# Retention in three fp32r passes, and the turn of the PSUM banks moved behind held values, in a two-block mixer

## What is computed

```python
p = h @ w_in                                  # q, k, v and gate of every head
q_l, k_l = rope(q_l), rope(k_l)               # latent tokens only
o_c, s_f, s_b = retention_bidir(q_c, k_c, v_c, lg_f, lg_b, zeros, zeros)
o_l, _, _     = retention_bidir(q_l, k_l, v_l, lg_f, lg_b, s_f, s_b)
# retention: out_n = sum_m gamma^|n-m| (q_n . k_m) v_m, forward and backward
on = o * rsqrt(mean(o * o) + EPS)             # per head, over the 512 values
y  = (on * norm_gain * silu(g)) @ w_out
```

## Time and profile before

| | before |
|---|---|
| median of three runs | 3357.47 us (3341.77 to 3360.63) |
| the profiled execution | 3363.55 us |
| its span | 3362.2 us |
| mean granted clock of TensorE | 0.988 of 2.4 GHz |
| busy: TensorE, VectorE, ScalarE | 3257.1, 1705.7, 1263.1 us |
| moved by DMA | 508.93 MB, mean 151 GB/s |
| retention heads | about 206 to 1830 us of the span |

### The profile page before, as it was taken

The page is one execution under the profiler, slowest core; times in us unless marked ns, Lnnn a source line. Parts: engine busy times, 40 slices in busy tenths (PEclk is TensorE's granted clock), DMA queues, the critical chain, the costliest instruction groups (busy, mean ns, idle before and its releaser), DMA issues.

```text
span 3362.2 us, 47886 instructions
## 1 busy us (share of the span) xinstructions
PE 3257.1 (97%) x20354; PEld 2788.5 (83%) x20354; DVE 1705.7 (51%) x2481; ACT 1263.1 (38%) x1803; POOL 0.2 (0%) x4
## 2 busy tenths in 40 slices
PE   7999999999999999999998999999999999999998
PEld 5677777777777777787875789988999999999998
DVE  5443443334334343443335567778676665555555
ACT  4342222222222222222223455556554444444443
POOL 0000000000000000000000000000000000000000
PEclk9999999999999999999998999999999999999999
DMA  9844423233332233323234234444545545555554
GB/s 371 307 157 182 163 100 131 89 125 125 109 129 94 107 119 114 131 107 113 107 113 163 94 125 139 151 138 158 197 165 173 175 154 166 173 186 189 185 187 144
DMA packets 153923, 508.93 MB, mean 151 GB/s; under 512 B 15344, under 2 KB 35952, under 8 KB 152944
## 3 DMA queue, kind: packets, MB, share of 16 engines
q1 hardware_dynamic: 149328, 493.03, 42.3%
q10 hardware_dynamic: 4384, 12.85, 1.0%
HBM read 501.62 MB, written 4.19 MB: 150 GB/s over the span
## 4 chain that ended last, share of the span: by engine, by line
PE 91%; DVE 3%; ACT 2%; DMA 2%; issue 1%; SPq 1%; ACTq 0%; DVEq 0%
PE bank L543 27%; PE bank L545 27%; PE bank L544 26%; PE bank L605 3%; PE bank L704 2%; PE bank L789 1%; DMA raw<-stream 1%; PE bank L770 1%; PE bank L690 1%; DVE w_lo L1561 1%; PE bank L706 1%; DMA raw_h<-stream 1%; SPq L516 1%; PE bank L780 1%; PE bank L621 0%
## 5 line engine op out<-in xcount | busy, mean ns | idle before, releaser
L543 PE MATMUL bank<-h_hi,w_hi 128*128 128x256 f32 (+1 forms) x4032 | 1271.2, 315 | 10.0 <-DVE w_lo L1561 9.5
L545 PE MATMUL bank<-h_hi,w_lo 128*128 128x256 f32 (+1 forms) x4032 | 1248.4, 310 | 0.0
L544 PE MATMUL bank<-h_lo,w_hi 128*128 128x256 f32 (+1 forms) x4032 | 1248.3, 310 | 0.0
L1561 DVE TENSOR_TENSOR w_lo<-raw,w_hi 128x1024 fp32r<-128x1024 f32 x731 | 885.3, 1223 | 659.7 <-ACT w_hi L1011 654.7
L1011 ACT ACTIVATE w_hi<-raw 128x1024 fp32r<-128x1024 f32 x731 | 764.2, 1057 | 976.4 <-PE bank L545 595.3
L543 PEld LDWEIGHTS bank<-h_hi,w_hi 128*128 128x128 f32 x4032 | 759.4, 188 | 83.9 <-issue 34.7
L545 PEld LDWEIGHTS bank<-h_hi,w_lo 128*128 128x128 f32 x4032 | 763.9, 189 | 43.5
L544 PEld LDWEIGHTS bank<-h_lo,w_hi 128*128 128x128 f32 x4032 | 761.7, 189 | 45.7 <-issue 3.6
L543 PE MATMUL bank<-w_hi,h_hi 128*128 128x512 f32 x704 | 289.6, 411 | 22.1 <-DVE w_lo L1561 9.4
L545 PE MATMUL bank<-w_hi,h_lo 128*128 128x512 f32 x704 | 278.4, 395 | 0.0
L544 PE MATMUL bank<-w_lo,h_hi 128*128 128x512 f32 x704 | 277.9, 395 | 0.0
(11 more groups left out here) (234 smaller groups left out, 2698.8 us busy)
## 6 DMA issues: line engine op xcount, KB each, us to landing
raw<-stream SPq DMA_DIRECT2D x904, 512.0 KB, 4.1
raw_h<-stream SPq DMA_DIRECT2D x32, 512.0 KB, 11.1
res<-tokens_in ACTq DMA_DIRECT2D x4, 1024.0 KB, 8.8
vg<-mem_in ACTq DMA_DIRECT2D x4, 512.0 KB, 9.1
h_hi<-mem_kv ACTq DMA_DIRECT2D x2, 1024.0 KB, 9.9
out<-res SPq DMA_DIRECT2D x4, 512.0 KB, 3.0
mem_kv<-qk ACTq DMA_DIRECT2D x1, 1024.0 KB, 4.8
mem_kv<-vg ACTq DMA_DIRECT2D x1, 1024.0 KB, 11.2
```

The source lines that it names most:

```text
L543: pe.matmul(out, sh, mh, start=start, stop=False)
L544: pe.matmul(out, sh, ml, start=False, stop=False)
L545: return pe.matmul(out, sl, mh, start=False, stop=stop)
L1561: dve.tensor_tensor(in_quarters(m.w_lo[slot][:, :]), m.raw[SLOT[raw]], in_quarters(m.w_hi[slot][:, :]).bitcast(F32), ALU.subtract).then_in ...
```

## The change

The class `Banks` gets a method that drops several held banks and sets the turn behind the last of them. It is used for all held values:

```diff
+    def drop_all(self, what, tiles):
+        for t in range(tiles):
+            self.drop(*what, t)
+        self.turn = self.values[(*what, tiles - 1)][0] + 1
...
-            for t in range(4):
-                banks.drop("v", h + 1, t)
+            banks.drop_all(("v", h + 1), 4)
```

Queries, keys, scores and values of the retention are split into high and low parts, and their products go through `product`. On TensorE:

```diff
-        pe.wait_ge(*s["roped"].at(h, 3))
+        pe.wait_ge(*s["q_lo"].at(h, 3))
         for mt in range(2):
+            keys = slice(L + mt * P, L + (mt + 1) * P)
             for dt in range(2):
-                mm = pe.matmul(outs[mt][:, :], m.qk[:, 2 + dt, L + mt * P:L + (mt + 1) * P], m.qk[:, dt, :],
-                               start=dt == 0, stop=dt == 1)
+                mm = product(outs[mt][:, :], (m.q_hi[:, 2 + dt, keys], m.q_lo[:, 2 + dt, keys]),
+                             (m.q_hi[:, dt, :], m.q_lo[:, dt, :]), dt == 0, dt == 1)
...
         def outputs_of_head():
-            pe.wait_ge(*banks.at("s", h, 2))
+            pe.wait_ge(*s["s_lo"].at(h, "lat"))
             pe.wait_ge(*banks.at("v", h, 3))
...
-                    pe.matmul(out[:, :], m.v[:, 2 + mt, dv], m.s_ctx[:, mt, :], start=mt == 0, stop=mt == 1)
+                    product(out[:, :], (m.v_hi[:, 2 + mt, dv], m.v_lo[2 + mt][:, dv]),
+                            (m.s_ctx_hi[:, mt, :], m.s_ctx_lo[:, mt, :]), mt == 0, mt == 1)
...
-                    mm = pe.matmul(out[:, LAT], m.v[:, mt, dv], m.s_lat[:, mt, :], start=False, stop=mt == 1,
-                                   skip_group_check=True)
+                    mm = product(out[:, LAT], (m.v_hi[:, mt, dv], m.v_lo[mt][:, dv]),
+                                 (m.s_lat_hi[:, mt, :], m.s_lat_lo[:, mt, :]), False, mt == 1, skip_group_check=True)
```

The latent scores change in the same way as those of the context. On ScalarE, the high parts:

```diff
+    def values_high(h):
+        act.wait_ge(s.mm, WHERE["v", h][7] + 1)
+        for t in range(4):
+            act.activation(m.v_hi[:, t, :], psum("v", h, t)[:, :], ACT.Copy).then_inc(*s["v_hi"].up(h, t))
...
+        def query_high(j):
+            act.wait_ge(*s["roped"].at(h, j))
+            act.activation(m.q_hi[:, j, :], m.qk[:, j, :], ACT.Copy).then_inc(*s["q_hi"].up(h, j))
         for j in range(4):
             ahead(("qk", h, j))
             swap((h, j), m.tmp[j % 2], m.qk[:, j, LAT], 64, banks.at("qk", h, j))
             beside(h, "t", j)
+            if j:
+                query_high(j - 1)
+        query_high(3)
...
         for j in range(3):
+            if j == 2:
+                for mt in range(2):
+                    act.wait_ge(*banks.at("s", h, mt))
+                    act.activation(m.s_ctx_hi[:, mt, :], m.s_raw[:, mt, :], ACT.Copy).then_inc(*s["s_hi"].up(h, mt))
+                act.wait_ge(*banks.at("s", h, 2))
+                act.activation(m.s_lat_hi[:, :, :], m.s_lat_raw, ACT.Copy).then_inc(*s["s_hi"].up(h, "lat"))
             tanh(("g", h, j), m.g[:, j, :], BOTH)
```

On VectorE, the low parts; the value banks are now given free by them:

```diff
+    def values_low(h):
+        for t in range(4):
+            dve.wait_ge(*s["v_hi"].at(h, t))
+            dve.tensor_tensor(m.v_lo[t][:, :], psum("v", h, t)[:, :], m.v_hi[:, t, :].bitcast(F32), ALU.subtract
+                              ).then_inc(*banks.up("v", h, t))
...
+        def query_low(j):
+            dve.wait_ge(*s["q_hi"].at(h, j))
+            dve.tensor_tensor(m.q_lo[:, j, :], m.qk[:, j, :], m.q_hi[:, j, :].bitcast(F32), ALU.subtract
+                              ).then_inc(*s["q_lo"].up(h, j))
...
+        dve.wait_ge(*banks.at("s", h, 2))
+        for mt in range(2):
+            dve.wait_ge(*s["s_hi"].at(h, mt))
+            dve.tensor_tensor(m.s_ctx_lo[:, mt, :], m.s_raw[:, mt, :], m.s_ctx_hi[:, mt, :].bitcast(F32), ALU.subtract
+                              ).then_inc(*s["s_lo"].up(h, mt))
+        dve.wait_ge(*s["s_hi"].at(h, "lat"))
+        dve.tensor_tensor(m.s_lat_lo[:, :, :], m.s_lat_raw, m.s_lat_hi[:, :, :].bitcast(F32), ALU.subtract
+                          ).then_inc(*s["s_lo"].up(h, "lat"))
```

`query_low(j - 1)` stands after the rotation of tile j, `query_low(3)` after the loop, `values_low(h + 1)` after the eight value chunks. In `normed_of_head` the four normalizations no longer stand before the four low parts; the low part of tile j comes two normalizations behind:

```diff
-            for j in range(4):
-                dve.tensor_tensor(m.g[:, j, :], m.g[:, j, :], m.o_rstd[:, :], ALU.mult).then_inc(*s["o_normed"].up(h, j))
-            for j in range(4):
-                dve.wait_ge(*s["o_hi"].at(h, j))
...
+            for j in range(6):
+                if j < 4:
+                    dve.tensor_tensor(m.g[:, j, :], m.g[:, j, :], m.o_rstd[:, :], ALU.mult).then_inc(*s["o_normed"].up(h, j))
+                if j >= 2:
+                    dve.wait_ge(*s["o_hi"].at(h, j - 2))
```

More of the change, by code:

```diff
@@ L335 @@
     "bias1", "squared", "sq_sum", "meaned", "rstd", "h_raw", "h_mod", "h_hi", "h_lo", "mv_turned",
-    "swapped", "roped", "decay_arg", "decay_exp", "decay", "tanh", "gate", "scored", "weighed",
+    "swapped", "roped", "q_hi", "q_lo", "s_hi", "s_lo", "v_hi", "decay_arg", "decay_exp", "decay", "tanh", "gate", "scored", "weighed",
     "o_out", "o_squared", "o_summed", "o_meaned", "o_normed", "o_hi", "o_lo", "added",
@@ L391, in __init__ @@
         self.tab = sb("tab", [P, TABLES_N])
+        v_lo_at += [nc.sbuf_base + 4 * T * i for i in range(3)]
         self.sq = [sb(f"sq{i}", [P, T]) for i in range(2)]
@@ L418, in __init__ @@
         self.o_lo = sb("o_lo", [P, 4, T], F32R, line=128)
-        self.tmp = [sb(f"tmp{i}", [P, L]) for i in range(2)]
+        tmps = sb("tmps", [P, 2, L], line=64)
+        tmp_at = at[0] - 4 * 2 * L
+        self.tmp = [tmps[:, i, :] for i in range(2)]
         self.o_rstd = sb("o_rstd", [P, T])
@@ L430, in __init__ @@
         self.raw += [x[:, 4 * i:4 * i + 4, LAT] for x in self.raw_h for i in range(4)]
-        self.v, self.g = self.vg[:, 0:4, :], self.vg[:, 4:8, :]
+        self.g = self.vg[:, 4:8, :]
+        self.q_hi, self.q_lo = [nc.alloc_sbuf_tensor_at(f"q_{x}", [P, 4, T], F32R, offset=o_at + 4 * 4 * T * i)
+                                for i, x in enumerate(("hi", "lo"))]
+        self.s_ctx_hi = nc.alloc_sbuf_tensor_at("s_ctx_hi", [P, 2, T], F32R, offset=s_at)
+        self.s_ctx_lo = nc.alloc_sbuf_tensor_at("s_ctx_lo", [P, 2, T], F32R, offset=decay_at)
+        self.s_lat_lo = nc.alloc_sbuf_tensor_at("s_lat_lo", [P, 2, L], F32R, offset=tmp_at)
+        self.v_hi = nc.alloc_sbuf_tensor_at("v_hi", [P, 4, RET_DV], F32R, offset=vg_at)
+        self.v_lo = [nc.alloc_sbuf_tensor_at(f"v_lo{t}", [P, RET_DV], F32R, offset=x) for t, x in enumerate(v_lo_at)]
+        self.s_raw, self.s_lat_raw = self.qk[:, 0:2, :], self.qk[:, 2, :].rearrange("p (a b) -> p a b", a=2)
         self.mem_raw = self.vg[:, :, :].rearrange("p a (b c) -> p (a b) c", c=L)
@@ L539, in weights, with product @@
         return m.w_hi[Q[c] % SLOTS], m.w_lo[Q[c] % SLOTS]
-    def product(out, stat, moving, start, stop):
+    def product(out, stat, moving, start, stop, **checks):
         (sh, sl), (mh, ml) = stat, moving
-        pe.matmul(out, sh, mh, start=start, stop=False)
-        pe.matmul(out, sh, ml, start=False, stop=False)
-        return pe.matmul(out, sl, mh, start=False, stop=stop)
+        pe.matmul(out, sh, mh, start=start, stop=False, **checks)
+        pe.matmul(out, sh, ml, start=False, stop=False, **checks)
+        return pe.matmul(out, sl, mh, start=False, stop=stop, **checks)
     def tile(what, cols, k_tiles=KT, k0=0, acts=None, between=None):
@@ L664, in tensor_program @@
                 mean("x0", BOTH)
-        for t in range(2):
-            banks.drop("mv", n, t)
+        banks.drop_all(("mv", n), 2)
     outs = values_banks(("v", 0), 4)
@@ L675, in tensor_program @@
         beside("start", "v", c)
-    for t in range(4):
-        banks.drop("v", 0, t)
+    banks.drop_all(("v", 0), 4)
     for h in range(RET_HEADS):
@@ L895, in tensor_program @@
                 mm.then_inc(*s["meaned"].up("x2_means"))
-        for t in range(2):
-            banks.drop("bv", n, t)
+        banks.drop_all(("bv", n), 2)
     pe.wait_ge(*s["h_lo"].at(2, KT - 1))
@@ L1766, in vector_program @@
             beside(h, "t", 4 + j)
+        dve.wait_ge(*s["q_lo"].at(h, 3))
         dve.wait_ge(*s["scored"].at(h, "ctx"))
```

41 lines of the change are left out of this document (24 added, 17 removed).

## The result

| | before | changed |
|---|---|---|
| median of seven runs | 3357.47 us (3341.77 to 3362.00) | 3321.64 us (3304.12 to 3330.62) |
| ratio | | 0.9887, 95% interval 0.9865 to 0.9909 |
| the profiled execution's span | 3362.2 us | 3320.3 us |
| busy: TensorE, VectorE, ScalarE | 3257.1, 1705.7, 1263.1 us | 3227.0, 1759.7, 1294.9 us |

What follows compares the result with a forecast made beforehand. TensorE's passes plus its few standstills were taken as the bound. Products 24.8 us and bank turn 9.7 gave 34.5 us off 3363.55, so 3329.0, scaled to a median of 3323 us; range 3307 to 3345.

Steps and rivals of the forecast that it cites:

- The pace of the passes: Scores and outputs: three fp32r passes replace each fp32 product, 12.38 us a head for 15.48, saving 24.8 us in eight heads.
- The rule that a quarter would fall away: Scores and outputs: dropping one of four passes would alone save 3.87 us a head, 31.0 us in all.
- The turn: Start of output projections: moving the bank turn past dropped value banks removes seven waits of 1.38 us, saving 9.7 us.
- rival (a): Bank turn gives nothing, as other waits replace those on the values' copies: 24.8 us saved, 3333 us; chance 0.12.
- The parts on ScalarE and VectorE: Seven more copies and eleven subtractions a head cost 0; the queue at the scores has 7.7 us of cover.
- signs of being wrong: New TensorE waits on w_lo inside heads, q_lo or s_lo, 256-column passes above 0.13 us, or a third-pair projection wait.
- v(0): Wait of 5.2 us between memory values and first value chunk: at most 0.8 us to be had, taken as 0.
- The sum: Whole kernel: 24.8 us from the products plus 9.7 from the turn, 34.5 us saved; bounds 28 to 42.
- (b): Weight loads set the pace of 256-column passes: 20.4 us lost, 14.1 saved, 3343 us; chance 0.05.
- (c): Scores and outputs: passes at 0.215 us, as the fourth-pass rule has it: 40.7 us saved, 3317 us; chance 0.07.
- (d): Small new waits at q_lo, s_lo or weights, 1 to 2 us a head: 18 to 27 saved, 3331 to 3340; 0.13.
- (e): Queue at the scores makes g(3)'s weights late, then TensorE runs at 1.2 GHz: 21 us slower, 3379 us; chance 0.05.

Runs made afterwards that it cites:

- e6: Changed kernel with the low by high pass left out of all scores and outputs, two runs: head period 194.11 us, ratio to before 0.9774.
- e4: Changed kernel with 20 useless ScalarE copies ahead of the third high part of the scores: head period 206.1 us, ratio to before 1.0066.
- e10: The changed kernel run once more, unaltered: median 3325.20 us, head period 198.29 us, ratio to before 0.9910.
- e12: Kernel before with nine tiny fp32 products put into the last block: median 3345.80 us, ratio to before 0.9981.
- e11: Changed kernel with the first gated tile ahead of the sums and nine tiny fp32 products in the last block: median 3307.62 us, ratio to before 0.9875.
- e1: Kernel before with only the bank turn moved (drop_all), scores and outputs still fp32: head period 201.19 us, ratio to before 0.9982.
- e3: Changed kernel with the four normalizations ahead of the four low parts again: head period 198.29 us, ratio to before 0.9909.
- e9: Changed kernel with VectorE gating the first output tile ahead of the sums, all heads but the last: head period 198.29 us, ratio to before 0.9887.
- e2: Changed kernel without the line that moves the turn: head periods 200.6 and 202.2 us in turn, ratio to before 0.9964.
- e7: Changed kernel with VectorE gating the first output tile ahead of the sums, all heads but the last: head period 198.29 us, ratio to before 0.9897.
- e8: Changed kernel with a tiny fp32 product ahead of each of 64 tiles of the last block: head period 198.29 us, ratio to before 0.9915.

## Why the prediction was right, point by point

**The pace of the passes.** 12.38 us a head were worked out for the new products; the blocks take 4.29 and 8.49 (533.75 to 542.24), 12.78. A dozen passes at the head of a block run at 0.23 to 0.24 instead of 0.227, the first takes 0.33. The old blocks were 0.2 us dearer than the sum too: 5.08 and 10.24 us by their starts, and the first fp32r pass behind each takes 0.42 us in place of 0.23. Saved: 2.90 us a head (201.19 - 198.29) where 3.10 were expected, 23.2 us in eight heads for 24.8. The rule that a quarter would fall away (31.0) is refused by the period: the 0.012 us by which each fp32r pass is longer than a quarter of the fp32 product are real. The prediction's 0.215 is that quarter, 0.86 divided by four, so it does not confirm four passes by itself; what the trace shows is two instructions of 0.43 to a product. Weight loads set nothing (e6).

**The turn.** 1.46 us a head for the 1.38 expected, and what comes last next was indeed nothing. What the prediction did not see is that the other part of the change lengthens the very wait that the turn removes. Its rival (a), in which the turn gives nothing, was priced at 24.8 us saved; the products without the turn saved 1.2 us a head, some 10 us by the periods and 15 by the medians. The sum came out right since both parts were there; the price of the rival was more than twice what the products gave alone.

**The parts on ScalarE and VectorE.** Eleven more subtractions and seven more copies a head cost nothing, and the one queue that could have hurt had the cover that the trace of before gave it, 7.7 against 7.6 us measured in the trace and 7.7 by e4. Nothing waits on q_lo or s_lo. Of the prediction's signs of being wrong one showed, in small: the changed kernel's trace has one new wait on w_lo inside a head, 0.39 us at 373.09 in head 0; e10's trace has none there.

**v(0).** The wait fell from 5.22 to 4.42 us, by the 0.8 that the prediction allowed at most, and h_lo comes last, as it said. That the 0.8 is met to the digit is luck: the same wait lasted 3.8 to 5.3 us in the other traces with the turn moved. The prediction took 0, since transfers follow, and nothing more can be said: the first query tile started between 220.05 and 226.66 us in the fourteen traces, with the turn in its new place as early as 220.05 and as late as 226.66. The 5.7 us there between the two first traces are no more than this scatter.

**The sum.** 34.5 expected; 33.3 in the heads by the first two traces, 33.2 by those of e12 and e11. It is made of 23.2 from the products (24.8 expected) and 7 x 1.46 = 10.2 from the turn (9.7 expected). The span fell by 41.9 because of 5.7 in the first stretch and 2.9 behind the heads. The latter is scatter as well: with the longer pace of the last block, that part took 1573.5 to 1578.8 us in eight traces (the changed kernel, e1, e3 to e6, e9, e10) and 1576.9 in that of the kernel before. That the median, 3321.64, came within 1.4 us of 3323 is in part luck, since it depends on how many of seven executions ran at the shorter pace. **The rivals** (b), (c), (d) are refused by the periods, (e) was real but 7.7 us away.

## What to carry to other kernels

A product in three fp32r passes is worth its splitting where TensorE is the bound and the pace of both forms is read from starts, not from record lengths: here 0.68 for 0.86 us at 512 columns and 0.35 for 0.43 at 256. When a value must pass two engines before its PSUM bank is free, look where the next bank in turn lies; a stop of 2 us cost more than its length in four heads of seven (e2), because TensorE ran at 1.2 GHz behind it. Taking a stop away can therefore save more than the stop: 5.4 us for 3.54 in e7. A round-robin that skips held buffers is worth starting behind them once they are dropped; here that gave 1.46 us a head alone and 3.1 with the products.

## What the runs showed that was not expected

Streams of fp32r passes of 256 columns run at one of two paces, 0.113 or 0.118 us, at the same granted clock of 1.00, and can keep it for hundreds of microseconds; the passes of 512 columns showed 0.227 in all traces. The pace nearly always changed where something else came between, once without (2782.3 us in the kernel before). Of the tiny fp32 products put into the stream, seven met the longer pace: four left it as it was, and three (one each in e8, e11, e12) turned it to the shorter. None of the 75 that met the shorter pace brought the longer back. Why there are two paces, and what decides whether a break turns one into the other, is not settled; no run tells it apart.

And the granted clock fell behind some stops of one length and not behind others. A stop of 2.06 us was followed by passes at 1.2 GHz in every second head of e2, stops of 1.22 us in none. The stop of 3.54 us in head 0 was followed by seven to twelve slow passes in ten traces and by none in e1. That is a piece of luck in e1's trace, whose heads together are 12.2 us shorter than before, 2 more than seven times 1.46.
